# The begin of a two-block transformer kernel rebuilt: loads in halves, the norm's factors applied in token rows

## The chip, the cores and the metric

The kernel runs on one NeuronCore of one Trainium2 chip. The metric is the device time of one execution in microseconds. The kernel before takes 1398.87 us (median of 3 runs, 1398.53 to 1399.31). The profiled execution is one run of its own: 1398.66 us, with a span of 1396.9 us from its first to its last instruction.

## What is computed

x is 256 tokens by 1024 features in fp32. Two transformer blocks follow each other; only the first stage of the first block matters here:

```python
h = rmsnorm(x, g_mix)                   # x / sqrt(mean(x*x) + eps) * g_mix, per token
proj = h @ w_in                         # w_in is 1024 x 4804
q_s, k_s, v_s, q_d, ..., q_m = proj[:, :1732] (split; several parts get rope)
m = rmsnorm(mem, g_mem)                 # mem is 256 x 1024
mkv = m @ w_mem_kv                      # 1024 x 512
gates = sigmoid(proj[:, 1732:] + b_gate)
...                                     # three attentions, gated sum, w_out, MLP, then block two
```

Every product is done as three passes over split operands: an operand is rounded to a high part (hi, type fp32r) and the rest (lo), and hi*hi + hi*lo + lo*hi is summed in PSUM.

## The kernel before

**Weights.** All weights are streamed as 1 MB units (128 partitions x 2048 values, that is 8 k-tiles x 256 columns for an up projection). SyncE loads a unit into one of three ring slots (`load`, L697) and waits for the slot's last reader. ScalarE rounds it to hi (`round_unit`, L1610), VectorE subtracts for lo (`low_unit`, L2105), in three split buffers; a few units have their lo made by GpSimd (`BY_POOL`). TensorE then waits for `split_ready`. The order of units is `plan_units`: proj 0 to 6 (the first 1732 columns of w_in; unit 6 has 196 columns), memkv 0 and 1, gate 0 to 11, and so on.

**Products.** `up_tok_split` (L850) does one tile: for each of 8 k-tiles three products with 128 tokens stationary and 256 weight columns moving, 24 in all. A unit has two tiles, b = 0 and 1, one for each 128 tokens. Results go to PSUM banks 0 to 3 in rotation (`plan_tiles`); a bank is opened only after its last tile was read (`open_tile`). The tile p(i, b) of unit i is read by ScalarE into `proj` (`copy_streams`, L1696).

**The norm of x (n = 0).** The rows of x come in two transfers of 512 KB, one for each 128 tokens, then unit proj 0. VectorE takes mean and variance (L2127 to L2130), ScalarE the root (`deviation`, L1629), VectorE the reciprocal and the scaled rows `xn` (L2138). TensorE transposes the 1024 features of 128 tokens in 8 transposes (`norm`, L956). The gain g_mix is applied after the transposition, where it is a per-partition scalar: it must itself be turned first. ScalarE's queue issues nine small loads of rows (gains, biases, encodings; L1600 to L1608), TensorE turns them in 10 transposes (tile `vec`), VectorE copies them to `colv`, and then ScalarE and VectorE apply the gain and split the result (`turned` with `gain` and `round_half`, L1656; `norm_turned`, L2140). SyncE holds back the loads of const, proj 1 and proj 2 until the nine row loads have landed (L760).

**The norm of mem (n = 1)** is done the same way between units 4 and 5: VectorE's `norm_rows(1)` stands between the lo parts of units 5 and 6, TensorE's `norm(1, b)` behind the tiles of unit 4, and its gain again on the turned tiles.

**Start.** `keep_warm` issues bf16 products over zeros that nobody reads: 12 before the first transposes, 6 before unit 0's products.

All engines work through their lists strictly in the order in which the code of each engine's block writes them. ScalarE's order at the begin: deviation(0, 0), deviation(0, 1), hi of proj 0, the turned x norm with hi of proj 1 inside, hi of proj 2, then for each unit i its two tile copies and the hi of unit i + 3, with the roots of the mem norm after i = 2 and its turned part at i = 4. VectorE's: `norm_rows(0)`, colv, lo of proj 0, `norm_turned(0)`, lo 1, lo 2, rope's angles, lo 3, 4, 5, `norm_rows(1)`, lo 6, `norm_turned(1)`, lo of memkv 0, rope.

Of the kernel before, what the change touches and what calls it, by code (L numbers as in the profile page):

```python
# [21 lines left out]
F32 = mybir.dt.float32  # L22
# [18 lines left out]
WARM_FIRST = 6  # L41
WARM_START = 12
# [33 lines left out]
V_GMIX, V_GMEM, V_GMLP, V_GFIN, V_LNG, V_LNB, V_BG, N_VEC = 0, 1, 2, 3, 4, 10, 16, 19  # L76
# [54 lines left out]
def plan_tiles():  # L131
# [23 lines left out]
    names += half_norm(0, 0) + [("vec",)] + half_norm(0, 1)  # L155
    names += [("p", i, b) for i in range(5) for b in range(NB)] + norm(1)
# [64 lines left out]
BY_POOL = SECOND | {("pdm", 1)}  # L221
# [105 lines left out]
def two_blocks(nc, t, out):  # L327
    ctx = ExitStack()
    with ctx:
# [71 lines left out]
        hT_tmp = act_out[:].rearrange("p a (x s) -> p (a x) s", x=2)  # L401
# [20 lines left out]
        b1_rows = take(at, P, of=shared_rows)[0:4]  # L422
        roped = take([0], NB, R_COLS, of=shared_rows)
# [69 lines left out]
        hT_rounded, hT_ready = sem("hT_rounded"), sem("hT_ready")  # L493
        tile_done = sem("tile_done")
        tile_read = [sem(f"tile_read{i}") for i in range(8)]
        x_in = [sem(f"x_in{b}") for b in range(NB)]
# [161 lines left out]
        def _(sp):  # L658
            for b in range(NB):
                sp.dma_start(resid[:, b, :], t["x"][0, b * P:(b + 1) * P, :]).then_inc(x_in[b], 16)  # L660
# [98 lines left out]
            load(("proj", 0))  # L759
            sp.wait_ge(vec_in, 16 * 9)  # L760
            sp.dma_start(const[:, P:N_CONST], t["consts"][:, P:N_CONST]).then_inc(const_in, 16)
            load(("proj", 1))
            load(("proj", 2))
            sp.dma_start(memt, t["mem"][0].rearrange("(b p) d -> p b d", p=P)).then_inc(mem_in, 16)
# [39 lines left out]
        def _(pe):  # L804
# [45 lines left out]
            def up_tok_split(o, unit, n, b, norm=None, act=both_hT, turns=None, hidden=None):  # L850


                for k in range(KT):
                    if norm is not None:
                        normed(norm, b, k)
                    if turns is not None and k in (4, 6):
                        turn_rows(turns, 1, (k - 4) // 2)
# [62 lines left out]
            def turn_rows(n, b, h):  # L920

                rows = xn if n == 2 else resid
# [26 lines left out]
            def keep_warm(n):  # L949


                nil = zeros[:, :].bitcast(BF16)
                for _ in range(n):
                    settle(mm(acc[0][:, :], nil[:, 0:P], nil[:, 0:512], True, True))

            def norm(n, b):  # L956
                pe.wait_ge(xn_ready, 4 * n + 2 * b + 2)
                for h in range(2):
                    o = open_tile(("n", n, b, h))
                    for k in range(4):  # L960
                        ins = turn(o[:, k * P:(k + 1) * P], xn[:, b, (h * 4 + k) * P:(h * 4 + k + 1) * P])
# [1990 lines left out]
```

## Time and profile before

| | |
|---|---|
| median of 3 runs | 1398.87 us |
| profiled execution, device time | 1398.66 us |
| its span | 1396.9 us |
| TensorE busy | 1364.2 us |
| VectorE busy | 938.3 us |
| ScalarE busy | 657.8 us |
| mean granted TensorE clock | 0.995 |

The page lists the busy time of each engine; the span less TensorE's busy time is what TensorE idles. A timeline row shows the start, the duration, the engine (a q behind it is its instruction queue), the line, the operation, and in brackets how long the engine was idle before and what ended that. Rows of one group that overlap are merged into one, with their count (x8). The first digits of a windows row are the stretch, then busy time and count of each engine, then the granted TensorE clock.

### The profile page before, as it was taken

The page shows a single profiled execution, that of the slowest core. Times are in us where ns is not written, and L with a number is a line of the kernel's source. Part 1 is how long each engine was busy: PE and PEld are TensorE (multiplying, and loading weights), DVE is VectorE, ACT ScalarE, POOL GpSimd, SP SyncE. Part 2 cuts the span into 40 slices and gives each one's busy share as a digit, 9 for nine tenths or more (in the row PEclk, how much of TensorE's full clock was granted, in tenths as well). Part 3 has the DMA queues.
Part 4 walks back from the last instruction along what each step waited for, and adds up shares of the span by engine and source line. Part 5 has one row for each costly group of instructions (what it writes and reads, how often), then busy time and mean ns, then how long its engine had stood idle before and what let it go on. Part 6 is the DMA issues. An engine that isn't in the chain of part 4 may idle for free.

```text
span 1396.9 us, 25172 instructions
## 1 busy us (share of the span) xinstructions
PE 1364.2 (98%) x10394; PEld 1274.9 (91%) x10394; DVE 938.3 (67%) x1372; ACT 657.8 (47%) x833; POOL 76.5 (5%) x73
## 2 busy tenths in 40 slices
PE   8999989999999999999999999999999999999997
PEld 7989978999999999999889999999999887899996
DVE  6778687656675555768885556666565667765566
ACT  5666544443443444454443434444433568543432
POOL 0000150000100000000030000100000200100000
PEclk8999999999999999999999999999999999999999
DMA  8434564776658767555466656766656530566551
GB/s 284 152 122 152 196 206 154 236 237 208 214 188 249 268 206 231 181 187 176 159 217 202 203 190 217 259 216 212 210 184 207 159 135 17 182 216 205 197 195 60
DMA packets 191526, 268.41 MB, mean 192 GB/s; under 512 B 5741, under 2 KB 164753, under 8 KB 191183
## 3 DMA queue, kind: packets, MB, share of 16 engines
q1 hardware_dynamic: 186336, 250.05, 54.6%
q0 software_dynamic: 4224, 15.91, 3.3%
q10 hardware_dynamic: 878, 1.21, 0.4%
q8 instruction: 64, 1.05, 0.3%
q14 instruction: 24, 0.19, 0.0%
HBM read 261.92 MB, written 4.19 MB: 190 GB/s over the span
## 4 chain that ended last, share of the span: by engine, by line
PE 80%; DVE 12%; ACT 4%; issue 1%; DMA 1%; POOL 0%; SPq 0%; DVEq 0%; ACTq 0%
PE bank L808 79%; DVE split L2113 2%; PE bank L831 1%; DVE stats L2181 1%; DVE resid L2207 1%; DVE resid L2215 1%; ACT split L1622 1%; DMA ring<-in_w_in 1%; DVE resid L2176 1%; ACT arena L2003 1%; DVE arena L2330 0%; ACT act_out L2012 0%; DVE best L2329 0%; DVE hT_lo L2225 0%; ACT act_out L1645 0%
## 5 line engine op out<-in xcount | busy, mean ns | idle before, releaser
L2113 DVE TENSOR_TENSOR split<-ring,split 128x2048 fp32r<-128x2048 f32 x217 | 496.0, 2288 | 310.8 <-ACT split L1622 309.8
L808 PE MATMUL bank<-hT_hi,split 128*128 128x256 f32 (+1 forms) x3984 | 683.8, 276 | 1.5 <-DVE hid_lo L2491 0.7
L808 PEld LDWEIGHTS bank<-hT_hi,split 128*128 128x128 f32 (+1 forms) x3984 | 611.0, 192 | 7.9 <-issue 4.7
L1622 ACT ACTIVATE split<-ring 128x2048 fp32r<-128x2048 f32 (+1 forms) x224 | 427.1, 1908 | 297.6 <-PE bank L808 292.9
L808 PE MATMUL bank<-hT_lo,split 128*128 128x256 f32 (+1 forms) x1992 | 547.8, 275 | 0.0
L808 PEld LDWEIGHTS bank<-hT_lo,split 128*128 128x128 f32 (+1 forms) x1992 | 381.7, 192 | 1.3
L808 PE MATMUL bank<-split,hid_hi 128*128 128x512 f32 x992 | 271.2, 380 | 1.6 <-DVEq L2495 1.0
L808 PEld LDWEIGHTS bank<-split,hid_hi 128*128 128x128 f32 x992 | 183.3, 189 | 25.4 <-issue 1.9
L808 PE MATMUL bank<-split,hT_hi 128*128 128x256 f32 (+2 forms) x896 | 168.5, 290 | 2.3 <-ACT act_out L1645 0.6
L808 PE MATMUL bank<-split,hid_lo 128*128 128x512 f32 x496 | 151.4, 379 | 0.0
L808 PEld LDWEIGHTS bank<-split,hT_hi 128*128 128x128 f32 x896 | 142.2, 193 | 8.5 <-issue 4.7
L1797 ACT ACTIVATE act_out<-bank 128x256 f32<-128x256 f32 (+1 forms) x104 | 43.4, 417 | 176.9 <-PE bank L808 176.8
L808 PE MATMUL bank<-split,hT_lo 128*128 128x256 f32 (+2 forms) x448 | 126.3, 288 | 0.0
L808 PEld LDWEIGHTS bank<-split,hid_lo 128*128 128x128 f32 x496 | 93.8, 189 | 13.2
L808 PEld LDWEIGHTS bank<-split,hT_lo 128*128 128x128 f32 x448 | 86.7, 193 | 1.3
L2818 POOL TENSOR_TENSOR split<-ring,split 128x2048 fp32r<-128x2048 f32 x7 | 32.4, 4626 | 711.0 <-ACT split L1622 500.1
L2459 DVE TENSOR_TENSOR hid_lo<-hid,hid_hi 128x256 fp32r<-128x256 f32 (+1 forms) x112 | 51.4, 459 | 3.8
L808 PE MATMUL bank<-arena 64*128 64x256 f32 (+6 forms) x442 | 50.2, 321 | 1.2 <-DVE neg_max L2701 0.8
L2560 DVE SCALAR_TENSOR_TENSOR hid<-act_out,bank 128x256 f32<-128x256 f32 x82 | 37.5, 458 | 19.7 <-ACT act_out L1797 19.7
L808 PEld LDWEIGHTS bank<-arena 64*128 64x128 f32 (+3 forms) x442 | 36.6, 168 | 10.9 <-issue 3.7
L2457 DVE CAST hid_hi<-hid 128x256 fp32r<-128x256 f32 (+1 forms) x112 | 34.9, 311 | 3.9
L1677 ACT ACTIVATE hT_hi<-bank 128x512 fp32r<-128x512 f32 x28 | 16.7, 598 | 39.9 <-PE bank L831 39.9
(217 smaller groups left out, 913.8 us busy)
## 6 DMA issues: line engine op xcount, KB each, us to landing
ring<-in_ffn_w SPq DMA_DIRECT2D x132, 1024.0 KB, 5.3
ring<-in_w_in SPq DMA_DIRECT2D x19, 1024.0 KB, 5.5
ring<-in_w_mlp_in SPq DMA_DIRECT2D x16, 1024.0 KB, 5.9
ring<-in_w_mlp_out SPq DMA_DIRECT2D x16, 1024.0 KB, 5.0
ring<-in_sgu_w_in SPq DMA_DIRECT2D x16, 1024.0 KB, 5.4
ring<-in_sgu_w_out SPq DMA_DIRECT2D x8, 1024.0 KB, 4.9
ring<-in_kv_w SPq DMA_DIRECT2D x6, 1024.0 KB, 5.8
ring<-in_w_out SPq DMA_DIRECT2D x4, 1024.0 KB, 4.9
```

Source lines behind the costliest of these rows:

```text
L808: ins = pe.matmul(o, lhsT, rhs, start=start, stop=stop)
L831: return pe.transpose(o, a, ident[0:n, 0:n])
L1622: act.activation(halves(q if i is None else q + BODY, n)[0], ring[:, u % SLOTS, 0:n], ACT.Copy).then_inc(hi_ready, 1)
L1677: act.activation(hT_hi[:, 4 * h:4 * h + 4, b * P:(b + 1) * P], o[:, :].rearrange("p (k s) -> p k s", k=4), ACT.Copy).then_inc(hT_rounded, 1)
L1797: act.activation(act_out[:, b, 0:cols], banks[b][:, 0:cols], func).then_inc(act_ready, 1)
L2003: ins = act.activation(s, s, ACT.Exp, bias=neg_max[:, m, k:k + 1], scale=-1.0, accum_out=row_sum[:, m, k:k + 1])
L2113: dve.tensor_tensor(lo, ring[:, u % SLOTS, 0:n], hi.bitcast(F32), ALU.subtract).then_inc(split_ready, 1)
L2176: link(dve.scalar_tensor_tensor(out=r, in0=r, scalar=ALPHA if n >= 4 else 1.0, in1=from_streams(acc[2 * b + h][:, :]), op0=ALU.mult, op1=A ...
L2457: dve.tensor_copy(hi, raw).then_inc(hid_rounded, 1)
L2459: return dve.tensor_tensor(lo, raw, hi.bitcast(F32), ALU.subtract)
L2560: dve.scalar_tensor_tensor(out=in_order(raw), in0=from_streams(act_out[:, b, 0:S]), scalar=0.5, in1=from_streams(banks[b][:, S:2 * S]), op ...
L2818: pool.tensor_tensor(lo, ring[:, u % SLOTS, :], hi.bitcast(F32), ALU.subtract).then_inc(split_ready, 1)
```

## The change

The begin of the kernel is rewritten on all engines. Behind memkv 0 only the place of the gate biases in `colv` changes.

- **Loads.** x's first 128 rows come in two halves of 512 features, then unit proj 0 in two halves of four k-tiles each, then the second 128 rows in two halves, proj 1, proj 2, const, three row loads (b_gate, compression bias and encodings) and mem, all issued by SyncE without the hold. ScalarE's queue issues only g_mix's row and the identity. The rows of the other gains are no longer loaded here. GpSimd loads g_mem broadcast to all partitions.
- **The x norm.** TensorE multiplies a row of ones by g_mix's row (two 128x512 fp32 products with one contraction row), which puts g_mix on all partitions in PSUM banks 4 and 5. VectorE scales the token rows by rstd and that gain in one instruction per half. The transposed tile is then final: ScalarE rounds it to hi and VectorE subtracts for lo straight from PSUM.
- **Unit 0.** Its hi is made in halves by ScalarE, its first lo half by VectorE, the second by GpSimd. Its products run by halves of k: four hi*hi, four hi*lo, four lo*hi, then the same for the other four k-tiles.
- **Order.** Tiles go (0,0), (1,0) with the second x transposes inside, (0,1), (1,1), then units 2 to 6. The mem transposes stand inside unit 4's tiles, and the turned rows (`vec`, now 3 + bias + encodings) behind unit 4.
- **Warm-up products:** 9, then 3 behind the spread of g_mix, then 4 behind the first transposes.

```diff
-WARM_FIRST = 6
-WARM_START = 12
+WARM_START = 9
+WARM_TURN = 3
+WARM_FIRST = 4
...
-    names += half_norm(0, 0) + [("vec",)] + half_norm(0, 1)
-    names += [("p", i, b) for i in range(5) for b in range(NB)] + norm(1)
+    names += half_norm(0, 0) + [("p", 0, 0)] + half_norm(0, 1) + [("p", 1, 0), ("p", 0, 1), ("p", 1, 1)]
+    names += [("p", i, b) for i in range(2, 4) for b in range(NB)]
+    names += half_norm(1, 0) + [("p", 4, 0)] + half_norm(1, 1) + [("p", 4, 1), ("vec",)]
...
-BY_POOL = SECOND | {("pdm", 1)}
+BY_POOL = SECOND | {("pdm", 1), ("proj", 0)}
... SyncE
+            load_first(0)
+            load_first(1)
+            for h in range(2):
+                load_x(1, h)
             load(("proj", 1))
             load(("proj", 2))
... TensorE
+            def spread_gain():
+                pe.wait_ge(g_mix_in, 16)
                 for h in range(2):
+                    settle(mm(acc[h][:, :], ones[:, :], g_mix_row[:, h * 512:(h + 1) * 512], True, True
+                              ).then_inc(g_mix_ready, 1))
...
+            def first_unit(b):
+                for h in range(2):
+                    ks = range(4 * h, 4 * h + 4)
+                    pe.wait_ge(hi_ready if h else first_hi, 1)
+                    pe.wait_ge(hT_rounded, 2 * b + h + 1)
+                    for k in ks:
+                        mm(o[:, 0:UC], hT_hi[:, k, rows], two_streams(unit[0][:, k, :]), k == 0, False)
+                    if h:
+                        have(("proj", 0))
+                    else:
+                        pe.wait_ge(first_lo, 1)
+                    for k in ks:
+                        mm(o[:, 0:UC], hT_hi[:, k, rows], two_streams(unit[1][:, k, :]), False, False)
+                    tile_copied(pe, ("n", 0, b, h))
+                    for k in ks:
+                        ins = mm(o[:, 0:UC], hT_lo[:, k, rows], two_streams(unit[0][:, k, :]), False, k == KT - 1)
...
             keep_warm(WARM_START)
+            spread_gain()
+            keep_warm(WARM_TURN)
             pe.wait_ge(ident_in, 16)
+            for h in range(2):
+                turn_rows(0, 0, h)
             keep_warm(WARM_FIRST)
+            first_unit(0)
+            proj_unit(1, 0, turns=0)
+            first_unit(1)
+            proj_unit(1, 1)
+            for i in range(2, N_PROJ):
                 for b in range(NB):
+                    proj_unit(i, b, turns=1 if i == 4 else None, turned_rows=b)
... ScalarE
             deviation(0, 0)
+            round_first(0)
+            round_turned(0, 0)
+            round_first(1)
+            round_unit(("proj", 1))
             deviation(0, 1)
+            copy_proj(0, 0)
             round_unit(("proj", 2))
+            round_turned(0, 1)
+            copy_proj(1, 0)
+            copy_proj(0, 1)
+            round_unit(("proj", 3))
+            copy_proj(1, 1)
+            act.wait_ge(angle_ready, 1)
+            act.activation(trig[:], ang[:, 2:4], ACT.Sin).then_inc(trig_ready, 1)
+            round_unit(("proj", 4))
+            for b in range(NB):
+                deviation(1, b)
+            ahead = ORDER[5:]
+            for i in range(2, N_PROJ):
                 for b in range(NB):
+                    if i == 4:
+                        round_turned(1, b)
+                    copy_proj(i, b)
                 round_unit(ahead.pop(0))
... VectorE
+            def scale_rows(n, b):
+                dve.wait_ge(sd_ready, NB * n + b + 1)
+                link(dve.reciprocal(rstd[:, b:b + 1], sd[:, b:b + 1]))
+                for h in range(2):
+                    cols = slice(h * 512, (h + 1) * 512)
+                    if n == 0:
+                        dve.wait_ge(g_mix_ready, h + 1)
+                    dve.scalar_tensor_tensor(out=xn[:, b, cols], in0=(memt if n else resid)[:, b, cols],
+                                             scalar=rstd[:, b:b + 1], in1=gain_bc[:, cols] if n else acc[h][:, :],
+                                             op0=ALU.mult, op1=ALU.mult).then_inc(xn_ready, 1)
...
+            rows_deviation(0, 0)
+            scale_rows(0, 0)
+            first_low()
+            for h in range(2):
+                low_turned(0, 0, h)
+            rows_deviation(0, 1)
+            low_unit(("proj", 1))
+            scale_rows(0, 1)
+            for h in range(2):
+                low_turned(0, 1, h)
+            low_unit(("proj", 2))
+            angles()
+            low_unit(("proj", 3))
+            dve.wait_ge(mem_in, 16)
+            rows_deviation(1, 0)
+            low_unit(("proj", 4))
+            dve.wait_ge(g_mem_in, 16)
+            scale_rows(1, 0)
+            rows_deviation(1, 1)
+            scale_rows(1, 1)
+            low_unit(("proj", 5))
+            for h in range(2):
+                low_turned(1, 0, h)
+            low_unit(("proj", 6))
+            for h in range(2):
+                low_turned(1, 1, h)
... GpSimd, behind its first two loads
+            pool.wait_ge(hi_ready, 1)
+            pool.wait_ge(first_lo, 1)
+            hi, lo = (r[:, 4 * UC:UNIT] for r in halves(0, UNIT))
+            pool.tensor_tensor(lo, ring[:, 0, 4 * UC:UNIT], hi.bitcast(F32), ALU.subtract).then_inc(split_ready, 1)
+            pool.dma_start(gain_bc, t["g_mem"][0].partition_broadcast(P)).then_inc(g_mem_in, 16)
```

## Rows read from the trace of the kernel before

**Rows 1.** The page, busy time of each engine.

```profile
PE 1364.2 (98%) x10394; PEld 1274.9 (91%) x10394; DVE 938.3 (67%) x1372; ACT 657.8 (47%) x833; POOL 76.5 (5%) x73
```

**Rows 2.** TensorE's waits from 0 to 130 us: total, times, longest.

```profile
PE bank L831 <- ACT arena L1698: 0.8, 1, 0.8
...
PE bank L808 <- ACT act_out L1645: 0.6, 1, 0.6
```

**Rows 3.** Timeline of all engines, 0 to 17 us.

```profile
0.82 0.86 SPq L660 DMA_DIRECT2D resid<-in_x  x2
...
1.39 5.06 PE L808 MATMUL bank<-zeros 128*128 128x512 bf16 x12 [1.39 <-POOL eps L2823]
...
8.05 1.06 PE L831 MATMUL bank<-const,xn 128*128 128x128 f32 x8 [1.60 <-DVE xn L2138]
...
10.05 1.06 SPq L710 DMA_DIRECT2D ring<-in_w_in  x2
...
11.04 1.97 PE L831 MATMUL bank<-const,xn 128*128 128x128 f32 x8
...
11.16 1.91 ACT L1622 ACTIVATE split<-ring 128x2048 fp32r<-128x2048 f32 x1 [1.24 <-DMA ring<-in_w_in]
...
13.11 2.29 DVE L2113 TENSOR_TENSOR split<-ring,split 128x2048 fp32r<-128x2048 f32 x1 [1.53 <-ACT split L1622]
...
16.15 0.55 PE L808 MATMUL bank<-split,hT_hi 128*128 128x256 f32 x1 [0.59 <-DVE hT_lo L2158]
```

**Rows 4.** Windows of 1 us: busy of each engine, clock, DMA share, GB/s.

```profile
3.00:4.00 1.00, 1.00 (x4) 0.38 (x3) 0.00 (x0) 0.00 (x0) 0.00 (x0) 1.00 1.03 404
...
9.00:10.00 1.00, 0.41 (x5) 0.30 (x4) 0.57 (x4) 0.29 (x1) 0.00 (x0) 0.74 0.60 192
...
19.00:20.00 1.00, 1.00 (x8) 1.00 (x7) 0.55 (x1) 1.00 (x3) 0.00 (x0) 0.64 1.02 406
```

**Rows 5.** Issue to landing of x's two transfers.

```profile
DMA to landing us min/median/max: 3.9/4.3/4.7
```

**Rows 6.** Timeline, 24 to 60 us: units 2 to 6 and the mem norm.

```profile
24.19 1.91 ACT L1622 ACTIVATE split<-ring 128x2048 fp32r<-128x2048 f32 x1 [0.32 <-DMA ring<-in_w_in]
...
25.15 0.16 DVE L2086 CAST pos_f<-pos_i 128x2 f32<-128x2 int32 x1
...
27.86 2.29 DVE L2113 TENSOR_TENSOR split<-ring,split 128x2048 fp32r<-128x2048 f32 x1
...
38.64 1.28 DVE L2127 BATCH_NORM_STATS2 stats<-shared_rows 128x6 f32<-128x512 f32 x2
...
40.45 0.29 ACT L1632 ACTIVATE sd<-msq,eps 128x1 f32<-128x1 f32 x1 [2.75 <-DVE msq L2130]
...
43.53 0.29 ACT L1632 ACTIVATE sd<-msq,eps 128x1 f32<-128x1 f32 x1 [2.79 <-DVE msq L2130]
...
44.26 1.91 ACT L1622 ACTIVATE split<-ring 128x2048 fp32r<-128x2048 f32 x1
...
59.02 5.55 PE L808 MATMUL bank<-two,split 128*128 128x256 f32 x48
64.73 5.62 PE L808 MATMUL bank<-split,two 128*128 128x256 f32 x48 [0.16 <-DVE split L2113]
```

**Rows 7.** Groups by shape: busy and mean ns of one.

```profile
L2225 DVE TENSOR_TENSOR hT_lo<-bank,hT_hi 128x512 fp32r<-128x512 f32 x28 | 19.4, 692 | 5.7 <-PE bank L808 3.5 <-ACT hT_hi L1677 1.7
...
L2215 DVE SCALAR_TENSOR_TENSOR resid<-resid,rstd,gain_rows 128x512 f32<-128x512 f32 x24 | 18.0, 752 | 0.8
...
L1677 ACT ACTIVATE hT_hi<-bank 128x512 fp32r<-128x512 f32 x28 | 16.7, 598 | 39.9 <-PE bank L831 39.9
```

**Rows 8.** GpSimd's subtractions, and GpSimd beside VectorE.

```profile
L2818 POOL TENSOR_TENSOR split<-ring,split x7: 4553/4634/4715, 170.8 to 1201.6; 128x2048 fp32r<-128x2048 f32 x7
...
194.99 0.79 POOL L2846 TENSOR_TENSOR shared_rows<-shared_rows 128x256 f32<-128x256 f32 x1
...
196.74 2.65 POOL L2846 TENSOR_TENSOR shared_rows<-shared_rows 128x256 f32<-128x256 f32 x1
```

More of the change, by code:

```diff
@@ L848, in up_T_split, with up_tok_split @@
                 return ins
-            def up_tok_split(o, unit, n, b, norm=None, act=both_hT, turns=None, hidden=None):
+            def up_tok_split(o, unit, n, b, norm=None, act=both_hT, turns=None, turned_rows=1,
+                             hidden=None):
                 for k in range(KT):
@@ L953, in keep_warm @@
                 for _ in range(n):
[L954 to L961, printed above, removed]
-                        if k == 0:
-                            settle(ins)
-                    ins.then_inc(tile_done, 1)
+                    settle(mm(acc[2][:, :], nil[:, 0:P], nil[:, 0:512], True, True))
@@ new lines, in proj_unit @@
+            def proj_unit(i, b, norm=None, **extra):
+                have(("proj", i))
+                n = min(UC, C_GATE - i * UC)
+                o = open_tile(("p", i, b))
+                up_tok_split(o[:, 0:n], parts(("proj", i), KT), n, b, norm, **extra).then_inc(tile_done, 1)
+                owed[0] += b
+            def first_unit(b):
+                unit = parts(("proj", 0), KT)
+                o = open_tile(("p", 0, b))
+                rows = slice(b * P, (b + 1) * P)
+                for h in range(2):
[6 more added lines that the diff above has]
+                        have(("proj", 0))
+                    else:
+                        pe.wait_ge(first_lo, 1)
[4 more added lines that the diff above has]
+                        ins = mm(o[:, 0:UC], hT_lo[:, k, rows], two_streams(unit[0][:, k, :]), False, k == KT - 1)
+                ins.then_inc(tile_done, 1)
+                owed[0] += b
@@ L986, in _ @@
-            norm(0, 1)
-            keep_warm(WARM_FIRST)
-            for i in range(N_PROJ):
-                have(("proj", i))
+            for h in range(2):
+                turn_rows(0, 0, h)
+            keep_warm(WARM_FIRST)
+            first_unit(0)
[3 more added lines that the diff above has]
+            for i in range(2, N_PROJ):
                 for b in range(NB):
-                    o = open_tile(("p", i, b))
-                    n = min(UC, C_GATE - i * UC)
-                    up_tok_split(o[:, 0:n], parts(("proj", i), KT), n, b, None if i else 0).then_inc(tile_done, 1)
-                owed[0] += 1
+                    proj_unit(i, b, turns=1 if i == 4 else None, turned_rows=b)
@@ L996, in _ @@
                 if i == 4:
-                    for b in range(NB):
-                        norm(1, b)
+                    pe.wait_ge(vec_in, 16 * 3)
+                    o = open_tile(("vec",))
+                    for k in range(KT):
+                        settle(turn(o[:, k * N_VEC:(k + 1) * N_VEC], vec_rows[:, k * P:(k + 1) * P], N_VEC))
+                    turn(o[:, V_B1:V_B1 + 4], b1_rows, 4)
+                    turn(o[:, V_PE:V_PE + 32], pe_rows, 32).then_inc(tile_done, 1)
             have(("memkv", 0))
@@ L2169, in add_rows, with first_low @@
+            def first_low():
+                dve.wait_ge(first_hi, 1)
+                hi, lo = (r[:, 0:4 * UC] for r in halves(0, UNIT))
+                dve.tensor_tensor(lo, ring[:, 0, 0:4 * UC], hi.bitcast(F32), ALU.subtract).then_inc(first_lo, 1)
             def add_rows(n, b, h):
```

179 lines of the change are left out of this document (49 added, 130 removed).

## The prediction, written before the result was known

> **What bounds the kernel now.** I read the page's busy times first, then TensorE's waits, then the timeline of the begin, and last the windows with the clock. The page shows TensorE busy for 1364.2 of the 1396.9 us of the span [rows 1]: the kernel is one long queue of products, and an edit is worth what it takes out of TensorE's idle time, out of its slow time, or out of its list. So the question is when TensorE starts a product that counts and what holds it up until memkv 0, the first unit behind the rewritten part. In the timeline the reader sees warm-up products from 1.39, transposes at 8.05 after 1.60 us of idle time, more at 11.04, and unit 0's first product at 16.15 [rows 3]. The chain to it: unit 0 landed at 11.14 (ScalarE's row waited for it), 1.91 us of hi, 2.29 us of lo, then the gain on the turned tiles. Behind 16.15 the only stalls up to memkv 0 are those of the mem norm, 0.8 and 0.6 us [rows 2]. memkv 0 starts at 59.02, and memkv 1 waits 0.16 us for its lo [rows 6]. Pace at the full clock: 48 products in 5.55 us with the last one's latency, so 0.112 us for one and 2.68 us for a tile of 24 [rows 6]; a transpose takes 1.06 / 8 = 0.13 us [rows 3]. At the low clock a transpose takes 1.97 / 8 = 0.246 us [rows 3], and I take a product at twice 0.107, 0.213 us. The granted clock fell within the ninth microsecond (0.74 there), after a stretch with little but 1.06 us of transposes, and came back within the nineteenth (0.64) [rows 4], some 3.5 us after the dense products of 16.15 began.
>
> **Start of the first products.** In the new order SyncE issues 0.52 MB of x, 1.05 MB of unit 0, 0.52 MB of x, then proj 1, each issue some 0.43 us (0.86 for two [rows 3]). x's first half million bytes landed 3.9 us after 0.82, at 4.7, the next 4.7 us after 1.26, at 6.0 [rows 5]: 0.42 MB/us. Later, proj 1, proj 2, const, mem and proj 3 (4.5 MB), the two units issued at 10.05 [rows 3], were all in at 24.17, when ScalarE stopped waiting for the last [rows 6]: counted from 12.3, about 0.38. I take 0.38. proj 1 is behind 2.62 MB more: 4.7 + 6.9 = 11.6, and 0.4 for the small loads of the other queues gives 12.0. Bounds: 11.2 at the 404 GB/s of the third microsecond [rows 4]; and 14.7 if the transfers lag as unit 0 did, which at 0.42 would have landed at 8.5 and landed at 11.14.
>
> ScalarE: hi of unit 0's first half (half of 1.91, 0.96), the two turned halves at 0.60 each [rows 7], hi of the second half until 10.9, hi of proj 1 from 12.0 to 13.95. GpSimd's half of lo costs half of 4.63, 2.3 us [rows 8], from 10.9 to 13.2; VectorE's lo of proj 1 waits for it and for hi, so it runs from 13.95 to 16.25. TensorE: nine warm-up products at 0.42 us [rows 3] to 5.2; the spread of g_mix has no like row; for two 512-column fp32 products I take 1.7 us, between 0.85 (two 512-column warm-up products) and 3.4 (four times that, one pass each for four). All of it is before 8.6, and the next thing late is ScalarE and the transfer, so it costs nothing. The scaled halves of x are at most 0.75 us each [rows 7] and come at 7.3 and 8.1; transposes end near 9.1; tile (0,0) runs from about 10, stalls for GpSimd until 13.2 and ends at 14.1. Then TensorE waits for proj 1: **tile (1,0) starts at 16.3**, 24 products (2.68 us) ahead of the kernel before. The removed row loads, ten transposes there and the gain passes pay only up to this point, since proj 1's transfer, hi and lo are what is late next.
>
> **From there to memkv 0** (in us after 16.3). TensorE's own list: 18 products and 8 transposes to the turned second rows of x, 3.05; the rest of (1,0) 0.67; (0,1) and (1,1) 5.36; units 2 and 3 10.7: tile (4,0) could open at 19.8. But it opens a bank whose last tile was p(3,0), and ScalarE copies that one only behind the roots of the mem norm and hi of proj 5. That chain goes through VectorE: turned rows 3.05; hi and lo of the second half 0.60 + 0.69 [rows 7]; lo 2 2.24; angles 2.7 (25.15 to 27.86); lo 3 2.24; stats of mem's first rows 1.8 (38.64 to 40.45); lo 4 2.24; gain and scale, reciprocal and two instructions by 0.7 [rows 7], 1.6; stats of the second rows 1.8; root and two copies 0.73 (43.53 to 44.26); hi 5 1.85; copy 0.35 [rows 6]. Sum 21.9: **TensorE idles 2.1 us before (4,0)**. Then (4,0) with its turns 3.73; 0.65 for VectorE's read of the turned tile whose bank (4,1) takes (hi 6 stands ahead of it on ScalarE); (4,1) 3.73; ten transposes of rows, moved here from the start, 1.3; units 5 and 6 10.75. memkv 0 starts at 16.3 + 42.05 = 58.35, against 59.02: **-0.67**. VectorE then is some 6 us ahead, so the wait of 0.16 before memkv 1 goes too: **-0.83**.
>
> The transposes of mem cost the same in both kernels; their two old stalls (1.4 us) are replaced by 2.75. The loads of mem, const, three rows and g_mem are queued behind proj 2: by 0.38 MB/us mem is in at 18 and proj 3 near 22.5, 0.5 us before ScalarE asks for it; without that cover each microsecond later costs one.
>
> **Clock.** Between 11.7 and 16.3 TensorE has 0.9 us of work. The one stretch like it in the trace, 6.45 to 9.5 with 1.06 us, brought the low level [rows 3, 4]. So (1,0) most likely runs at 1.2 GHz and gets 2.4 GHz some 3.5 us later: its first 18 products and 8 transposes cost 5.8 us at the low level, 3.5 us of it do 60%, the rest takes 1.2 us: 4.7 in place of 3.05, **+1.7**. Bounds: 0 if the level holds, 2.75 if it stays low through all of them. What is slow behind the turned rows is covered by the 2.1 us of idle time before (4,0). Sum: +0.9. The profiled execution's 1398.66 becomes 1399.6; the median of the runs shown is 0.2 above that execution: 1399.8.
>
> A rule against the halves: the DMA row above shows 404 GB/s with 512 KB transfers behind each other [rows 4]. The Trainium skill, "DMA: Bandwidth & Descriptors", section "Bandwidth", advises to batch to 1 MiB and gives 341 GB/s for that size; as an estimate from its figure proj 1 would land 0.8 us later and the time be 1400.6. The row decides, and I keep 0.38.
>
> **Rivals.**
> The clock holds (0.20). For: the clock was granted in full at 3 us and still for most of the ninth microsecond, in spite of 1.60 us of idle time before 8.05 [rows 3, 4]. Then the sum is -0.83: 1398.0.
> The mem norm is hidden (0.24): the two waits at unit 4, 2.75 us, don't arise because VectorE gets through its list before TensorE needs the bank. It needs the chain of 21.9 to be 2 us shorter, and the clock not to fall. For: many of its links are rounded up with their dispatch. Against: it is in ScalarE's and VectorE's lists in that order. -0.83 - 2.75 = -3.6: 1395.3.
> Transfers lag (0.14): the other side. proj 1 lands at 14.7 in place of 12.0, as unit 0 did with small loads beside it; three small row loads, two GpSimd loads and g_mem's broadcast are still there. It decides from a landing at 13.9 on. 2.7 more than the sum: +3.6, 1402.5.
> GpSimd is held by VectorE (0.05): a GpSimd subtraction of 0.79 us took 2.65 when VectorE subtracted beside it [rows 8]. Here VectorE would have to subtract from SBUF while GpSimd has its half: 1.9 us more, lo of proj 1 from 15.1, +1.2 to 1.6 on the sum, 1401.2. Against: VectorE reads the turned tile from PSUM then, and lo of proj 1 waits for GpSimd. By the Trainium skill, "SBUF — State Buffer", section "Who interferes with whom", the lock needs a VectorE instruction with two SBUF inputs; by that rule only the short variance step could meet it.
>
> **How the numbers follow.** The forecast (clock falls, both waits at unit 4) has 0.37, with its own range 1398.6 to 1401.3. 0.2% is 2.8 us, about what a measurement of this kernel can tell from no change. Faster by more: the hidden mem norm, 0.24. Slower by more: lagging transfers, 0.14. The other three are within, 0.62. The range from 1395.1 to 1401.8 leaves out the far half of the first and most of the second.
>
> **What would show it.** A wait of TensorE for lo of proj 1 ending near 16.3; a wait for ScalarE's copy before tile (4,0) of about 2 us; granted clock below 1 between 14 and 20; memkv 0's first product at 60.0, less 0.16 behind it. If (4,0) opens without a wait, the chain through VectorE is wrong. If proj 1 is ready before 15 or after 18, the transfers are. A change beyond unit 6 of more than 1 us would be one that I don't see.

## Result and the profile after

The changed kernel takes **1405.78 us** (median of 5 runs, 1402.64 to 1407.27) against 1398.87 (median of 5, 1398.53 to 1399.45): ratio 1.0040, interval 1.0029 to 1.0051. By the ratio it is slower by about 5.6 us, 0.4%. The prediction was 1399.8, 0.9 us slower, with a range up to 1401.8: the direction was right, and the size was not, by 4 us beyond the end of the range. The profiled execution took 1404.28 us, with a span of 1402.5.

The page of the kernel after, busy time of each engine, answers to [rows 1]:

```profile
PE 1368.0 (98%) x10396; PEld 1278.1 (91%) x10396; DVE 937.4 (67%) x1364; ACT 650.9 (46%) x814; POOL 79.5 (6%) x75
```

TensorE has 3.8 us more busy time with two instructions more. That alone doesn't say that products ran slowly, since the new spread of g_mix below is busy for 3.78 us; the clock in the windows further down does. TensorE's waits up to 130 us, against [rows 2]:

```profile
PE bank L825 <- DVE split L2129: 3.4, 2, 2.9
PE bank L825 <- ACT arena L1697: 1.9, 1, 1.9
...
PE bank L825 <- DVE two L2220: 0.8, 1, 0.8
PE bank L825 <- POOL split L2854: 0.7, 1, 0.7
```

The timeline of its begin, 0 to 24 us, against [rows 3]:

```profile
1.39 4.02 PE L825 MATMUL bank<-zeros 128*128 128x512 bf16 x9 [1.39 <-POOL eps L2835]
...
1.45 0.88 POOL L2848 DMA_DIRECT2D pos_i<-in_positions  x1
...
2.32 0.57 POOL L2850 DMA_DIRECT2D sinks<-in_sinks  x1
...
5.34 3.78 PE L825 MATMUL bank<-shared_rows,ones 1*128 1x512 f32 x4
...
10.22 1.06 ACT L1707 ACTIVATE split<-ring 128x1024 fp32r<-128x1024 f32 x1 [3.40 <-DMA ring<-in_w_in]
10.30 1.92 PE L848 MATMUL bank<-const,xn 128*128 128x128 f32 x8
...
13.36 1.37 PE L825 MATMUL bank<-split,hT_hi 128*128 128x256 f32 x8
...
13.88 2.41 POOL L2854 TENSOR_TENSOR split<-ring,split 128x1024 fp32r<-128x1024 f32 x1 [10.99 <-ACT split L1707]
...
15.21 1.10 DVE L2143 SCALAR_TENSOR_TENSOR msq<-mv 128x1 f32<-128x1 f32 x1
16.09 1.91 ACT L1654 ACTIVATE split<-ring 128x2048 fp32r<-128x2048 f32 x1 [2.29 <-DMA ring<-in_w_in]
...
18.03 2.29 DVE L2129 TENSOR_TENSOR split<-ring,split 128x2048 fp32r<-128x2048 f32 x1 [1.73 <-ACT split L1654]
...
20.38 0.55 PE L825 MATMUL bank<-split,hT_hi 128*128 128x256 f32 x1 [2.88 <-DVE split L2129]
```

The first products do come 2.8 us earlier than 16.15 [rows 3]. But ScalarE's row at 16.09 waited for proj 1's transfer: it landed at about 16.1, where the forecast had 12.0. Hi and lo follow, and tile (1,0) starts at 20.38. A second path was late too: GpSimd's half of lo ended at 16.29, where the forecast had 13.2, and VectorE's lo of proj 1 has to wait for it. The windows show what TensorE's clock did behind that gap and behind the next one (stretch, busy time and count of each engine, granted clock, DMA share, GB/s), as [rows 4]:

```profile
20.00:21.00 1.00, 0.62 (x3) 0.62 (x4) 0.96 (x3) 0.99 (x1) 0.00 (x0) 0.72 1.03 393
21.00:23.00 2.00, 2.00 (x11) 2.00 (x11) 0.84 (x2) 0.00 (x0) 0.00 (x0) 0.50 1.06 366
23.00:24.00 1.00, 1.00 (x7) 1.00 (x6) 0.00 (x0) 0.00 (x0) 0.00 (x0) 0.57 1.02 304
44.00:45.00 1.00, 1.00 (x7) 1.00 (x8) 1.00 (x1) 0.70 (x1) 0.00 (x0) 0.67 0.00 0
45.00:46.00 1.00, 1.00 (x7) 1.00 (x6) 0.76 (x1) 1.00 (x1) 0.00 (x0) 0.50 0.00 0
46.00:47.00 1.00, 1.00 (x7) 1.00 (x7) 0.00 (x0) 0.21 (x1) 0.00 (x0) 0.50 0.07 18
47.00:48.00 1.00, 1.00 (x7) 1.00 (x7) 0.16 (x1) 0.60 (x1) 0.00 (x0) 0.62 0.83 233
```

And TensorE's rows in the timeline at unit 4 and memkv 0, against [rows 6]:

```profile
43.86 0.35 PE L825 MATMUL bank<-split,hT_hi 128*128 128x256 f32 x1 [1.94 <-ACT arena L1697]
...
50.12 0.35 PE L825 MATMUL bank<-split,hT_hi 128*128 128x256 f32 x1 [0.83 <-DVE two L2220]
...
53.84 0.80 PE L848 MATMUL bank<-const,shared_rows 3*128 3x3 f32 x10
...
65.37 2.87 PE L825 MATMUL bank<-two,split 128*128 128x256 f32 x24
```

memkv 0 starts at 65.37 against 59.02 [rows 6]: **+6.35**. Behind it nothing more is lost: ScalarE's copies of the same tiles stand 6.0 us later at 131 us (125 before) and 5.9 later at 1349, and the span is 5.6 longer. The account, by the forecast's own steps: tile (1,0) 4.1 later than forecast; from (1,0) to (4,0) 23.5 where the forecast has 21.9 + 1.7; from (4,0) to memkv 0 21.5 where it has 20.15. Sum 4.1 - 0.1 + 1.35 = 5.3 over the forecast's 60.05.

### The profile page after: what moved, and what is told of

The parts are those of the page before. It is cut to its first block, busy times and chain, and to the rows that moved or that the text cites. A ratio compares the mean times of both kernels' runs of the same rounds, so it can differ in the third digit from the quotient of the medians.

```text
span 1402.5 us, 25164 instructions
## 1 busy us (share of the span) xinstructions
PE 1368.0 (98%) x10396; PEld 1278.1 (91%) x10396; DVE 937.4 (67%) x1364; ACT 650.9 (46%) x814; POOL 79.5 (6%) x75
## 3 DMA queue, kind: packets, MB, share of 16 engines
q8 instruction: 64, 1.05, 0.3%
## 4 chain that ended last, share of the span: by engine, by line
PE 81%; DVE 12%; ACT 4%; issue 1%; DMA 1%; POOL 0%; SPq 0%; DVEq 0%; ACTq 0%
PE bank L825 80%; DVE split L2129 2%; PE bank L848 2%; DVE stats L2175 1%; DVE resid L2201 1%; DVE resid L2209 1%; DVE resid L2170 1%; DMA ring<-in_w_in 1%; ACT split L1654 1%; ACT arena L2019 1%; DVE arena L2342 0%; ACT act_out L2028 0%; DVE best L2341 0%; DVE hT_lo L2220 0%; ACT hT_hi L1676 0%
## 5 line engine op out<-in xcount | busy, mean ns | idle before, releaser
L1654 ACT ACTIVATE split<-ring 128x2048 fp32r<-128x2048 f32 x223 | 425.0, 1907 | 298.8 <-PE bank L825 293.4
L2572 DVE SCALAR_TENSOR_TENSOR hid<-act_out,bank 128x256 f32<-128x256 f32 x82 | 37.5, 458 | 19.8 <-ACT act_out L1813 19.8
L825 PEld LDWEIGHTS bank<-arena 64*128 64x128 f32 (+3 forms) x442 | 36.7, 168 | 10.9 <-issue 3.7
```

What stands on the lines that cost most here:

```text
L825: ins = pe.matmul(o, lhsT, rhs, start=start, stop=stop)
L1654: act.activation(halves(q if i is None else q + BODY, n)[0], ring[:, u % SLOTS, 0:n], ACT.Copy).then_inc(hi_ready, 1)
L2572: dve.scalar_tensor_tensor(out=in_order(raw), in0=from_streams(act_out[:, b, 0:S]), scalar=0.5, in1=from_streams(banks[b][:, S:2 * S]), op ...
```

## Experiments

Each edit is on the changed kernel unless another is named. All were timed against the kernel before on the same chip; its median there was 1399.93 us beside e1 to e4, 1399.44 beside after_again and e5 to e7, 1400.22 beside e8 to e10 and 1399.34 beside e11. So times are best compared by their ratio to it. The starts of tiles are those of one profiled execution of each kernel. The transfers, the wait at unit 4 and the clock are the suspects.

**e1_hold: hold the transfers behind proj 1.**

```diff
             load(("proj", 1))
+            sp.wait_ge(arrived[1], 16)
             load(("proj", 2))
```

> The changed kernel, but SyncE issues proj 2, const, the row loads and mem only once proj 1 has landed. Theory I (transfers that are in flight together share the bandwidth, so that proj 1 lands with what was issued behind it): by the changed kernel's windows the 3.15 MB up to and with proj 1 are moved by 12.6 us, so proj 1 lands near 13.2 in place of 16.1, tile (1,0) starts near 17.5 in place of 20.4, and the time falls by 2 to 3 us to about 1402.5. Theory II (only the low rate of the first 8 us matters, order within the queue is kept): proj 1 lands at 16 as before, time 1405 to 1406.

Measured 1404.43 (1402.39 to 1406.19), ratio 1.0031 [1.0020, 1.0042]. proj 1 had landed by 13.69 in place of 16.1, and (1,0) started at 18.73, behind a wait of 1.24 us and without a fall of the clock. The transfers queued behind proj 1 do delay its landing. They delayed unit 0's first half as well: it was in at 6.98 in place of 10.2. But proj 2 and 3 come later: ScalarE waited 1.05 us for proj 3, the wait at (4,0) grew to 2.69, and from (1,0) to (4,0) it takes 22.59 us, where e4 below shows 21.83 with the same high clock. Some 0.8 us of the gain goes back to proj 3 in this way; memkv 0 is at 62.83.

With proj 1 in, its timeline shows what holds (1,0) next:

```profile
13.87 2.41 POOL L2855 TENSOR_TENSOR split<-ring,split 128x1024 fp32r<-128x1024 f32 x1 [10.99 <-ACT split L1708]
...
16.39 2.29 DVE L2130 TENSOR_TENSOR split<-ring,split 128x2048 fp32r<-128x2048 f32 x1
```

VectorE starts lo of proj 1 when GpSimd's half of unit 0 is done, at 16.3, although ScalarE's hi of proj 1 was ready at 15.6. In the changed kernel that half ended at 16.29 too, so with all else as it was, even a proj 1 that landed at 12.0 would have brought (1,0) no further forward than to about 18.7.

**e2_small_later: GpSimd issues its two small loads (positions 1 KB, sinks 4 KB) behind its half of lo.**

```diff
-            pool.dma_start(pos_i[:], ...)
-            pool.dma_start(sinks[:], ...)
             pool.wait_ge(hi_ready, 1)
 ...
             pool.dma_start(gain_bc, t["g_mem"][0].partition_broadcast(P)).then_inc(g_mem_in, 16)
+            pool.dma_start(pos_i[:], ...)
+            pool.dma_start(sinks[:], ...)
```

> The changed kernel, but GpSimd's two small loads (positions and sinks) are issued behind its half of unit 0's lo instead of at 1.4 us. Theory S (their small packets, 40% of the engines' time in the sixth microsecond, hold up the large transfers): the rate between 4 and 8 us rises from about 220 to 350 GB/s or more, unit 0's first half lands near 8.5 in place of 10.2, and proj 1 1 to 1.5 us sooner; time 1403.5 to 1405. Rival: the rate stays low because the large transfers themselves (1 KB packets, cold start) set it; landings and time stay, 1405 to 1406.

Measured 1402.99 (1400.27 to 1404.24), ratio 1.0017 [1.0007, 1.0026]. Two windows of 1 us, of the kernel after and then of this one, show the effect (DMA share and GB/s last):

```profile
4.00:5.00 1.00, 1.00 (x4) 0.23 (x2) 0.32 (x1) 0.00 (x0) 0.00 (x0) 1.00 0.81 155
...
7.00:8.00 1.00, 1.00 (x2) 0.33 (x1) 0.50 (x2) 0.00 (x0) 0.00 (x0) 1.00 0.88 236
```

```profile
4.00:5.00 1.00, 1.00 (x5) 0.41 (x4) 0.58 (x2) 0.00 (x0) 0.00 (x0) 1.00 0.99 292
...
7.00:8.00 1.00, 1.00 (x8) 0.51 (x7) 0.86 (x2) 0.97 (x1) 0.00 (x0) 1.00 1.09 412
```

And the queues of the kernel after between 6 and 7 us (packets, MB, share of the 16 engines' time):

```profile
q1 hardware_dynamic: 251, 0.25, 73.8%
q0 software_dynamic: 23, 0.00, 39.6%
```

23 packets of next to no bytes took 39.6% of the engines' time. Without them unit 0's first half was in at 6.9 in place of 10.2 and proj 1 at 12.8 in place of 16.1. (1,0) starts at 17.10, and memkv 0 at 62.39, 3.0 us earlier. The prediction had the small loads as "0.4 us"; they cost 3.

**e3_whole: x's rows and unit 0 in whole transfers**, 512 KB and 1 MB, the order unchanged.

```diff
-            load_first(0)
-            load_first(1)
-            for h in range(2):
-                load_x(1, h)
+            load(("proj", 0))
+            sp.dma_start(resid[:, 1, :], t["x"][0, P:2 * P, :]).then_inc(x_in[1][0], 16)
```

> The changed kernel with x in two whole transfers and unit 0 in one, in place of halves; the order of issue is kept. If the halves cost rate (smaller packets, more transfers), the rate between 3 and 5 us goes back to the 400 GB/s of the kernel before, x's first rows land at 4.7 in place of 5.3 and proj 1 lands 1 us or more sooner, time 1404 to 1405. If the halves are harmless, unit 0's hi starts later than 10.2 because all of it must land, proj 1 lands at 16.1 as before, and the time is the changed kernel's or up to 1 us more.

Measured 1403.02 (1400.97 to 1405.46), ratio 1.0022 [1.0013, 1.0032]. Unit 0 whole was in at 9.97, no later than its first half in the kernel after, and proj 1 at 14.29, 1.8 earlier; (1,0) starts at 18.58 and memkv 0 at 63.33, 2.0 earlier. With the small loads in flight, the halves of the transfers brought nothing here and cost 1.8 us of proj 1's landing. (In the four profiles with halves, small loads and units queued behind, it landed between 16.0 and 16.4.) For this place the advice of the Trainium skill, "DMA: Bandwidth & Descriptors", section "Bandwidth", to batch to 1 MiB agrees in direction, although bursts of 400 GB/s are seen with either size (400 from 9 to 10 us here, 412 from 7 to 8 us in e2).

**e4_warm_gaps: 13 products that nobody reads ahead of (1,0), 8 ahead of (4,0).**

```diff
             first_unit(0)
+            keep_warm(13)
             proj_unit(1, 0, turns=0)
 ...
+                if i == 4:
+                    keep_warm(8)
                 for b in range(NB):
```

> The changed kernel with warm-up products in its two largest gaps: 13 before tile (1,0), where TensorE waits 2.9 us, and 8 before tile (4,0), where it waits 1.9 us. Theory C (each gap makes the granted clock fall for about 3.3 us of products behind it): the clock stays at its high level from 20 to 24 and from 44 to 47.6, the two low stretches cost 1.6 and 1.4 us and are gone, time 2 to 3 us less, 1402.5 to 1404, and the spread between runs shrinks. Rival: zeros don't hold the clock, or the chain through VectorE and ScalarE gives the time back: 1405 to 1406.

Measured 1400.92 (1399.59 to 1403.25), ratio 1.0008 [0.9999, 1.0018]. TensorE in its timeline:

```profile
20.73 0.38 PE L825 MATMUL bank<-split,hT_hi 128*128 128x256 f32 x1 [0.43 <-DVE split L2132]
...
42.56 0.35 PE L825 MATMUL bank<-split,hT_hi 128*128 128x256 f32 x1 [0.19 <-ACT arena L1700]
...
62.43 5.55 PE L825 MATMUL bank<-two,split 128*128 128x256 f32 x48
```

The granted clock is 1.00 in every window up to 60 us. The waits for transfers and engines are all still there (filled, not removed), yet memkv 0 comes 2.9 us earlier, although (1,0) starts 0.35 later. From (1,0) to (4,0) it takes 21.83 us and not 23.48, from there to memkv 0 19.87 and not 21.51: that is what the two falls of the clock cost, 1.65 each. 21.83 is the chain of 21.9 of the prediction. The other profiles agree on the second fall: TensorE waits for the mem norm in each of the fourteen, and the clock fell behind that wait in the seven in which it was 1.94 us or more and in none of the seven in which it was 0.84 or less.

**after_again: the changed kernel unedited**, beside the next three.

> The changed kernel unaltered, beside the kernel before and the three runs of this call, since the runs of the first four experiments and those of the changed kernel were taken at different times. Expected 1404 to 1406, 4 to 6 us over the kernel before, with a spread of some 3 us that follows the clock.

1404.59 (1402.06 to 1407.78), ratio 1.0036 [1.0026, 1.0047]: (1,0) at 20.43, wait at (4,0) 1.94, (4,1) opened at 50.53. It has one thing that the first profile has not: its four products of the spread took 1.98 us and not 3.78, and the turned rows still cost 1.94, so (1,0) was as late. The spread is not on the path here.

**e5_act_order: ScalarE's second root of the mem norm behind the copies of unit 3.**

```diff
-            for b in range(NB):
-                deviation(1, b)
+            deviation(1, 0)
 ...
+                if i == 3:
+                    deviation(1, 1)
                 round_unit(ahead.pop(0))
```

> The changed kernel with ScalarE's list changed in one place: the second root of the mem norm stands behind the copies of unit 3 in place of ahead of unit 2's. Theory V (ScalarE held at that root is what keeps unit 3's tile in its bank, and the wait drops the clock): the wait of 1.9 us before tile (4,0) is gone and the low clock from 44 to 47.6 with it, memkv 0 starts 3.3 us earlier than in the changed kernel (62.1 in place of 65.4) and the time falls by 3. Rival: TensorE waits as long at tile (4,1) or at its transposes instead, since VectorE's list is the bound; then the time falls by less than 1 us.

1404.64 (1403.62 to 1406.01), ratio 1.0038 [1.0024, 1.0052]. The wait at (4,0) is gone and a wait of 2.24 us stands before (4,1). Its timeline shows why (VectorE's lo of unit 5, then its read of the turned tile; then TensorE):

```profile
45.26 2.28 DVE L2130 TENSOR_TENSOR split<-ring,split 128x2048 fp32r<-128x2048 f32 x1
47.47 1.28 DVE L2221 TENSOR_TENSOR two<-bank,two 128x512 fp32r<-128x512 f32 x2
...
48.89 0.35 PE L825 MATMUL bank<-split,hT_hi 128*128 128x256 f32 x1 [2.24 <-DVE two L2221]
```

TensorE asks for the turned tile sooner, VectorE reads it only behind lo 5, and the clock falls there instead (0.83 between 50 and 60 us). The rival of the expectation came: the time is that of after_again, and memkv 0 stands at 65.79 (65.78). One link taken out of a chain exposes the next.

**e6_before_warm: the kernel before with 17, 3, 3 and 18 warm products**, so that its clock stays high.

```diff
-WARM_FIRST = 6
-WARM_START = 12
+WARM_FIRST = 18
+WARM_START = 17
```

> The kernel before with its idle stretches at the begin filled by warm-up products: 17 in place of 12 at the start, 3 ahead of and 3 behind the turned rows, 18 in place of 6 ahead of unit 0. If the clock is what idle stretches cost, it is high at 16.15, unit 0 runs at 0.112 us for a product from the start, and the time is 1.7 us under the kernel before. Rival: the fillers run at the low clock themselves and push unit 0's start back to 18 or later; then the time is 0 to 3 us over.

1399.43 (1398.19 to 1400.67), ratio 0.9998 [0.9989, 1.0008]: nothing. The clock held, the turns of mem stood at 44.59 (44.73 before), since VectorE and ScalarE set their time. What a low clock costs depends on what sets the pace behind it: ten microseconds of it are nearly free in the kernel before (memkv 0 at 58.89 against 59.02), and 3.6 us of it behind (1,0) cost 1.65 in the changed one (e4).

**e7_all: e2, e5 and e4 together.**

> The changed kernel with three edits at once: GpSimd's small loads behind its half of lo, ScalarE's second root behind unit 3's copies, and warm-up products in the gaps before (1,0) and (4,0). By the parts: tile (1,0) starts at 17.1 with the clock high (in place of 20.4 at the low clock), no wait at (4,0). memkv 0 then starts near 57.5 to 58.5, 1 us before that of the kernel before, and the time is 0 to 2 us under the kernel before. If the edits don't add up, most likely since (4,1) or lo of proj 1 waits in their place, it is 1 to 2 us over it.

1400.30 (1397.90 to 1401.15), ratio 1.0002 [0.9992, 1.0012], memkv 0 at 61.31. Its first microseconds differ from e2's. In its timeline:

```profile
5.33 3.78 PE L825 MATMUL bank<-shared_rows,ones 1*128 1x512 f32 x4
...
13.69 1.92 ACT L1657 ACTIVATE split<-ring 128x2048 fp32r<-128x2048 f32 x1
...
16.38 2.29 DVE L2133 TENSOR_TENSOR split<-ring,split 128x2048 fp32r<-128x2048 f32 x1
...
17.56 2.75 PE L825 MATMUL bank<-zeros 128*128 128x512 bf16 x12
...
19.96 0.46 PE L825 MATMUL bank<-split,hT_hi 128*128 128x256 f32 x1
```

The slow form of the spread came back and ScalarE's hi of proj 1, at 13.69, waited for no transfer but for its own work on the turned rows. GpSimd's half ended at 16.28, and lo of proj 1 was ready at 18.7 (16.9 in e9, with the fast form). So the spread costs nothing only while transfers are later. (1,0) then started 1.3 us later still, at 19.96: TensorE was in its 13 warm products. And 8 more before (4,0), where the wait had gone, cost 1.7 us themselves. Without these 3.0 us memkv 0 would be at 58.3, within the 57.5 to 58.5 that was expected.

**e8_best: what the first seven point to.** Small loads later; the second root between the two copies of unit 3; VectorE's reads of the turned tiles ahead of lo 5 and lo 6; shorter warm-up ahead of the spread; 13 products ahead of (1,0).

```diff
-WARM_START = 9
-WARM_TURN = 3
+WARM_START = 5
+WARM_TURN = 2
...
+            keep_warm(13)
             proj_unit(1, 0, turns=0)
...
-            low_unit(("proj", 5))
             for h in range(2):
                 low_turned(1, 0, h)
-            low_unit(("proj", 6))
+            low_unit(("proj", 5))
             for h in range(2):
                 low_turned(1, 1, h)
+            low_unit(("proj", 6))
```

> The changed kernel with four edits: GpSimd issues the loads of positions and sinks behind its lo half of x; ScalarE's deviation of tile (1,1) stands between the two copies of unit 3; VectorE reads the turned tiles of the mem norm one step earlier, ahead of its lo halves of proj 5 and 6; 13 fp32 products that are read by nobody stand ahead of tile (1,0), and 5 and 2 instead of 3 and 1 of them ahead of the spread and of the turns. Theory (late landing of proj 1 plus the fixed chain of 21.9 us from tile (1,0) to tile (4,0), plus the wait for the turned tile): with the small loads out of the way tile (1,0) starts at 17.1 to 17.5 us, no wait over 0.3 us is left at (4,0) or (4,1), and memkv 0 begins at 56.5 to 57.5 against 59.02 before: 1397 to 1397.5 us. Rival (tile (1,0) is held by the halves of x and of unit 0 on VectorE and GpSimd, not by transfers): (1,0) stays at 18.5 or later and memkv 0 begins at 58.5 or later: 1399 to 1400. Second rival (the vec products or units 5 and 6 take up the gain, waiting for lo 5 or lo 6): memkv 0 at about 59: no change from before.

(The numbers of warm products that it replaces are 9 and 3, as the diff has them, and all of them are bf16 products over zeros.) Measured **1397.25** (1396.36 to 1399.35) against 1400.22, ratio 0.9981 [0.9972, 0.9990]: below the kernel before by an interval that excludes no change. Its timeline, TensorE:

```profile
17.83 0.46 PE L825 MATMUL bank<-split,hT_hi 128*128 128x256 f32 x1
...
38.99 0.60 PE L848 MATMUL bank<-const,xn 128*128 128x128 f32 x4
...
42.20 0.35 PE L825 MATMUL bank<-split,hT_hi 128*128 128x256 f32 x1 [0.83 <-DVE two L2222]
...
57.45 4.77 PE L825 MATMUL bank<-two,split 128*128 128x256 f32 x41
```

(1,0) at 17.83; (4,0) opens without a wait, 1.42 us ahead of the turns of mem at 38.99 as in the other kernels, at 37.6: 19.8 behind (1,0), TensorE's own list as the prediction summed it. The wait of 0.83 at (4,1) stays; the expectation had it gone. (1,0) is 0.3 us later than expected, and memkv 0 is at 57.45, the upper end. The edit changes several things at once, so this run doesn't say what each is worth. The ratio stands for 2.7 us, while memkv 0 is 1.57 us earlier than in the kernel before; where the rest comes from isn't shown.

**e9_small_warm: e2 and e4 together, and e10_small_hold: e2 and e1 together.**

> The changed kernel with the small loads behind GpSimd's lo half of x, and 13 products read by nobody ahead of tile (1,0), 8 ahead of tile (4,0). If the two edits remove separate terms (landing of proj 1, and low clock behind the two gaps), memkv 0 begins at 60.3 to 60.8 us (62.43 with the products alone, 62.39 with the small loads alone) and the time is 1399 to 1400. If the products only fill time that the late landing left open, it is no better than the products alone: memkv 0 at 62.4, 1401.

1400.15 (1399.04 to 1403.25), ratio 1.0006 [0.9997, 1.0016]; waits for lo of proj 1 0.6, at (4,0) 0.82, memkv 0 at 59.31, 3.1 earlier than with either edit alone: at memkv 0 the two terms add. It is then 0.3 from the kernel before's, and the time can't be told from it. The times alone don't show the sum: e4's ratio is 1.0008 [0.9999, 1.0018].

> The changed kernel with the small loads behind GpSimd's lo half of x, and SyncE issuing the load of proj 2 only when proj 1 has landed. If transfers queued behind proj 1 delay its landing by sharing the engines, proj 1 lands at about 12.0 us or earlier against 12.8 with the small loads alone. If what is left of the delay is the sum of bytes ahead of it, it lands at 12.8 again, and proj 2 and 3 come later by about 1 to 2 us. Time 1402 to 1404 either way, since the wait for proj 3's transfer comes back.

One run, 1404.16. Windows of this kernel:

```profile
10.00:11.00 1.00, 1.00 (x5) 0.42 (x3) 0.79 (x2) 0.74 (x3) 0.00 (x0) 0.50 1.10 349
11.00:12.00 1.00, 1.00 (x7) 0.70 (x6) 1.00 (x2) 0.81 (x1) 0.10 (x1) 0.73 0.72 233
12.00:13.00 1.00, 1.00 (x12) 1.00 (x11) 0.96 (x3) 0.00 (x0) 1.00 (x1) 1.00 0.06 20
```

ScalarE could start hi of proj 1 at 13.15: no sooner than the 12.80 of e2, although the engines had next to nothing else to move from about 11.7 on. (Without the small loads and without the hold it started between 12.69 in e9 and 13.32 in e8.) So with the small loads gone, transfers behind proj 1 no longer delay it. What is left is the sum of the bytes and a thin tail: the last 22 packets, 0.02 MB, took from 12.0 to about 12.6, and the landing followed half a microsecond later. The extra 3.3 us of the changed kernel need small loads in the queues and units queued behind, and halves instead of whole transfers add to them: each alone out of the way brings proj 1 to 12.8 (e2), 13.7 or earlier (e1) and 14.3 (e3). These gains overlap and can't be added up. Where in the engines the small packets hold the last part of a unit isn't shown by these profiles and stays open.

**e11_before_small: the kernel before with its small loads later.**

```diff
+            pool.wait_ge(cols_ready, 1)
             pool.dma_start(pos_i[:], ...)
```

> The kernel before, unchanged but that GpSimd issues the loads of positions and sinks only when VectorE has copied the turned vectors (at about 11.5 us) instead of at 1 us. It tells whether the gain of the repaired change (1397.25 against 1400.22) is that of the rebuilt begin or of the small loads alone. Theory (the rebuild brings it): the first hi part comes 1 to 2 us earlier than 11.16, but the first product still waits for VectorE's and ScalarE's work on the turned tiles, and the turns of mem stay bound by VectorE's and ScalarE's own lists: turns of mem at 44.2 to 44.8 (44.73 before), memkv 0 at 58.5 to 59.1, no change (1399 to 1400). Rival (the small loads cost the kernel before as much): the first product at 14.2 to 15.2 instead of 16.15, memkv 0 at 57 to 58, 1397.5 to 1398.5.

1398.51 (1397.93 to 1399.79), ratio 0.9994 [0.9985, 1.0003]. Between the two theories: hi of unit 0 at 10.28 (11.16 [rows 3]), first product 15.27 (16.15), turns of mem 43.74 (44.73), memkv 0 at 58.05, 1.0 us earlier; the interval doesn't exclude no change. So of e8's 1.6 us at memkv 0, about 1 could be had without the rebuilt begin. By the times the two can't be told apart: their intervals overlap.

## Why the prediction was wrong

- **The step that failed: "proj 1 is behind 2.62 MB more: 4.7 + 6.9 = 11.6, and 0.4 for the small loads of the other queues gives 12.0."** It landed at about 16.1. e10 and e2 split the miss: 0.8 to 1.1 us are left without the small loads, since the bulk of the bytes takes until about 12 and the tail and the landing another microsecond; 3.3 go with the small loads, which had "0.4" in the sum, and need units queued behind. The halves have their part in these 3.3: whole transfers land proj 1 1.8 us earlier (e3), where the prediction kept 0.38 against the rule for whole transfers that it had weighed. The upper bound of 14.7, taken from unit 0's lag of 2.6 us in the kernel before, had the right mechanism and was too low. The rival "transfers lag" was the case that came, at a chance of 0.14, and it too said 14.7 and 1402.5 where 16.1 and 1405.8 were measured. The prediction's own sign for this case, proj 1 ready after 18, came: its lo was ready at 20.3.
- **A second step, hidden by the first: "hi of the second half until 10.9" and GpSimd's half of lo "from 10.9 to 13.2".** The hi ended at 13.80 and GpSimd's half at 16.29, 3.1 late, while its length was right (2.41 for 2.3). ScalarE had unit 0's first half only at 10.2, and the spread and the transposes ran at the low pace, until 12.2. Either is enough for most of it: e1 has the half at 6.98 and the slow spread, and GpSimd ended at 16.28; after_again has the fast spread and the half at 10.2, and it ended at 15.7. This path alone puts (1,0) at 18.7 in place of 16.3 (e1), so 2.4 of the 4.1 us would have been lost with a timely proj 1 too.
- **The clock, first fall.** Forecast +1.7 behind the gap before (1,0); 23.5 - 21.9 = 1.6 measured, and confirmed by e4. Right in size. The forecast looked for it between 14 and 20; it came later, with the gap, in the microsecond from 20 on (0.72).
- **The clock, second fall: missed.** The prediction has TensorE idle 2.1 us before (4,0) and counts that time only as cover. The wait itself lowered the clock for the 3.3 us behind it, and there no idle time covers it: 1.35 over the forecast (1.65 by e4). The row that should have told it is the one used for the first gap [rows 4]; it was applied to one gap and not to the other that the same text forecast.
- **The chain of 21.9 from (1,0) to (4,0)**: 21.83 in e4. The wait of 2.1 at (4,0) was 1.94, with 0.65 at (4,1) at 0.83. Right; the rival "mem norm is hidden" did not come. In e8, with the order changed on two engines, the wait at (4,0) is gone and the one at (4,1) is not.
- **Spread of g_mix "costs nothing"**: right here, as proj 1's landing was later (after_again), but its size was wrong: 3.78 us, or 1.98 in other executions, against 1.7. In e7, with transfers early, it is on the path. Its slow form is also part of the second step above.
- **GpSimd held by VectorE**: the lock showed on VectorE instead. Its variance step on 128x1 took 1.10 us beside GpSimd's subtraction and ended with it, at 16.31 against 16.29; it takes 0.22 elsewhere (e7: 1.25 us beside it). By the Trainium skill, "SBUF — State Buffer", section "Who interferes with whom", the two engines contend only for a shared port pair, which is an exclusive lock, and a VectorE instruction meets it with two SBUF inputs, as this one has; the trace agrees. (The section names VectorE's two-port modes as a second way, which the prediction's sentence leaves out.) The lock cost nothing here, since lo of proj 1 waits for GpSimd's half and for a later hi in any case.
- **Behind memkv 0**: no new wait, as said.

Put together: 60.05 + 4.1 - 0.1 + 1.35 = 65.4. The median lies another 1.5 above the profiled execution. The profiles show a likely reason for the spread between runs, though not for this median: in eleven of the fourteen, after_again among them, there are some 3.3 us of low clock near 210 or near 1110 us (a window of 10 us reads 0.83), and in those of the kernels before and after and of e4 there are none.

## What to carry to other kernels

Count the waits that your own forecast makes: one of 2 us on TensorE in a dense stretch costs its length and can cost nearly as much again by the clock (1.65 us in e4). Products that nobody reads hold the clock in a wait, and cost their own length where the wait is shorter than they are (1.3 and 1.7 us in e7). A transfer's time at the start of a kernel is not bytes over bandwidth: look for tiny loads in flight on another queue, and move them behind the first large ones before anything is cut into halves (e2, e3, e11). When the last wait of a chain is explained, look at the path that would be last without it (e1). When the engines behind TensorE set its pace, taking out one wait moves it to the next reader (e5); e8 changes the order on two of them in one go.

## What had not been expected of the hardware

- Two loads of 5 KB in all took 39.6% of the DMA engines' time in one microsecond and, with units queued behind, delayed the landing of a 1 MB unit by 3.3 us.
- A transfer ends in a thin tail: in e10 the rate fell below 200 GB/s at 11.6 us, the last packets came near 12.6 and the landing at 13.1.
- At the begin the pace of TensorE differs from what the granted clock says: it is 1.00 in all windows from 2 to 14 us of the kernel after, yet 8 transposes took 1.92 us there (at 10.30), and 1.06 in the kernel before at 8.05 [rows 3]. The same program's four products of the spread took 3.78 us in one execution and 1.98 in another.
- Behind the wait of 1.94 us (ended at 43.86) TensorE ran some 3.3 us at the lower of its two levels, 1.2 GHz; behind the wait of 0.83 before (4,1) it kept 2.4 GHz in all ten profiles that have it. A wait of about 2 us doesn't always do it. Every profile of the study has the same wait of 2.20 us near 210 us, in the kernel before as

```profile
209.36 0.66 PE L831 MATMUL bank<-const,xn 128*128 128x128 f32 x4 [2.20 <-DVE xn L2213]
```

and the clock fell behind it in four of the fourteen (after_again, e2, e7 and e9) and stayed at 2.4 GHz in the others, the kernel before among them. What decides it isn't shown.
